# Routing four of five token tiles inside the last output product, with picks by counting, in a bidirectional RWKV-7 / GLA / expert trunk

## The reference, cut to what matters

```
x  = x + ga1 * (concat(y_rw, y_gla) @ w_out)
h2 = rmsnorm(x, norm2_g) * (1 + sc2) + sh2
g_logits = h2 @ moe_w_group + moe_b_group        # 4 groups
e_logits = h2 @ moe_w_expert + moe_b_expert      # 16 experts, 4 in a group
g_idx = argmax(g_logits); g_w = softmax(g_logits)[g_idx]
top_v, top_i = top_k(softmax(e_logits[group g_idx]), 2)
wts = g_w * top_v / sum(top_v)
x = x + ga2 * sum over the 2 picks of wts * (silu(h2 @ w3) * (h2 @ w1)) @ w2
```

## Time and profile before

| | us |
|---|---|
| median of 3 runs | 957.44 |
| lowest, highest of them | 954.83, 959.0 |
| span of the profiled execution | 963.3 |

### The profile page before, as it was taken

How to read it: one execution, slowest core, us unless ns; L and a number is a source line. 1 busy time by engine, 2 the same in 40 slices (tenths; PEclk the granted TensorE clock), 3 DMA queues, 4 the chain that set the end, 5 groups by cost and what they waited for, 6 DMA issues and landing times.

```text
span 963.3 us, 21505 instructions
## 1 busy us (share of the span) xinstructions
PE 868.1 (90%) x8900; PEld 533.8 (55%) x8900; DVE 562.5 (58%) x935; ACT 331.8 (34%) x583; POOL 151.6 (16%) x296
## 2 busy tenths in 40 slices
PE   2899999999999979888888988899976899999995
PEld 1455455666455436577777877545565444444442
DVE  3424046699986899365665656686244255444467
ACT  3231111142035664566666553122110122222223
POOL 7000111112000106122223420000001000000041
PEclk9999999999999989899999999999955899999998
DMA  9902222224253102112212121961019499999956
GB/s 331 378 23 95 94 88 99 89 88 154 75 188 109 67 1 42 26 21 53 39 37 34 32 38 47 314 254 44 22 54 361 133 328 373 367 371 368 327 126 226
DMA packets 120816, 142.46 MB, mean 148 GB/s; under 512 B 49996, under 2 KB 86280, under 8 KB 120328
## 3 DMA queue, kind: packets, MB, share of 16 engines
q1 hardware_dynamic: 111880, 116.55, 36.9%
q0 software_dynamic: 3744, 13.63, 4.5%
q10 hardware_dynamic: 5088, 10.82, 3.0%
HBM read 122.99 MB, written 18.00 MB: 146 GB/s over the span
## 4 chain that ended last, share of the span: by engine, by line
PE 79%; DVE 10%; DMA 5%; issue 3%; ACT 3%; SPq 0%; ACTq 0%; DVEq 0%; POOLq 0%
PE bank L1972 72%; PE bank L1976 7%; DMA region<-in_w_ada_dram 3%; DVE rk_r L1431 1%; ACT region L949 1%; DMA region<-in_w_in_dram 1%; DMA rk_r<-h_rows_dram,slot_tokens 1%; DVE region L1431 1%; DVE rk_r L1432 1%; DVE cl_b L1890 1%; DVE region L1961 1%; ACT w_sb L949 1%; ACT ada_row_buffers L949 0%; DVE region L1957 0%; DVE region L1943 0%
## 5 line engine op out<-in xcount | busy, mean ns | idle before, releaser
L1972 PE MATMUL bank<-region 64*64 64x64 f32 (+3 forms) x3900 | 402.6, 299 | 16.4 <-issue 6.5
L1972 PEld LDWEIGHTS bank<-region 64*64 64x64 f32 (+1 forms) x3900 | 233.3, 149 | 171.6 <-issue 160.1
L949 ACT ACTIVATE region<-bank 128x256 f32<-128x256 f32 (+3 forms) x216 | 97.8, 453 | 357.7 <-PE bank L1972 261.1
L1972 PE MATMUL bank<-region,rk_r 128*128 128x512 f32 x176 | 81.0, 615 | 0.8 <-issue 0.8
L1976 PE MATMUL bank<-ident,region 128*128 128x128 f32 (+2 forms) x403 | 63.6, 289 | 15.1 <-DMA region<-in_c_dram 11.1
L1976 PEld LDWEIGHTS bank<-ident,region 128*128 128x128 f32 (+2 forms) x403 | 46.0, 146 | 33.6 <-issue 24.0
L1942 DVE TENSOR_SCALAR region<-region 128x256 f32<-128x256 f32 x16 | 4.7, 295 | 101.3 <-ACT region L949 101.3
L1431 DVE SCALAR_TENSOR_TENSOR rk_r<-region,vec,rk_r 128x512 f32<-128x512 f32 x64 | 50.1, 783 | 11.1 <-ACT rk_r L949 9.0
L1972 PEld LDWEIGHTS bank<-region,rk_r 128*128 128x128 f32 x176 | 34.0, 198 | 40.2 <-issue 39.0
L924 POOL DMA_INDIRECT rk_r<-h_rows_dram,slot_tokens x16 | 15.2, 949 | 248.9 <-PE bank L1976 132.8
L1972 PE MATMUL bank<-scratch,region 64*64 64x64 f32 (+1 forms) x688 | 43.8, 232 | 6.3 <-issue 3.4
(11 more groups left out here) (279 smaller groups left out, 1149.0 us busy)
## 6 DMA issues: line engine op xcount, KB each, us to landing
region<-in_moe_w_dram SPq DMA_DIRECT2D x38, 1024.0 KB, 10.2
region<-in_w_ada_dram SPq DMA_DIRECT2D x12, 2048.0 KB, 9.0
region<-in_w_in_dram SPq DMA_DIRECT2D x6, 2048.0 KB, 9.1
cl_b<-in_moe_w_dram SPq DMA_DIRECT2D x10, 1024.0 KB, 12.6
expert_rows_dram<-yg_b ACTq DMA_DIRECT2D x14, 512.0 KB, 6.8
region<-late_condition_dram SPq DMA_DIRECT2D x3, 1024.0 KB, 9.4
a_rows_dram<-region SPq DMA_DIRECT2D x20, 128.0 KB, 2.7
region<-inverse_rows_dram SPq DMA_DIRECT2D x20, 128.0 KB, 3.1
```

The costliest lines, as they stand in the source:

```text
L949: return act.activation(out, in_, func, **kw)
L1972: return pe.matmul(out, lhsT, rhs, start=start, stop=stop)
```

## The change

1. **Tile order** is now [0, 3, 2, 1, 4].
2. **Shift's routing product.** POOL multiplies the routing weights by the columns of sh2 (`shift_w`, two operations), and PE multiplies them by a ones matrix: 8 products of 128x40, placed in the second tile's round (n = 1). VectorE reads bank `rc` there, and each tile's logits come out complete.
3. **Four tiles first.** In the last tile's round PE turns and routes the third and fourth tile between parts of `out` (4, 0); the four tiles' ranks are counted in the middle of `out` (4, 1), and most of their token products stand right behind it. x1, its transposes and h2 of the last tile come in two halves. Ranks, one-hot rows and ids of the last tile follow.
4. **Picks by counting** (`choose`). Each logit is compared with the others of its group (two comparisons, `beats`), masked so that ties go to the lower index, and summed. A logit beaten by none is first, one beaten by one is second.
5. **Weights of the picks** (`chosen_weights`, `pick_weights`, bank `sw`) come after the token numbers: VectorE works them out behind `slot_tokens`, PE forms `sw` within expert 0, after `turn_rows(1)`.
6. **Loads.** Weights of expert 1 start when `out` (4, 0) is done, those of expert 2 after the first three gathers have landed; w2 of expert 0 when the last mixer rows are turned. Buffers 2 and 3 are exchanged in w13 and in w2r. POOL's last gathers wait for `ug` 14, not 13.

The core of the diff:

```diff
@@ buffers
-        w13 = [ring[:, 1], ring[:, 0], cl_b[:, 0:SLAB].rearrange("p (k n) -> p k n", k=KT)]
+        w13 = [ring[:, 1], cl_b[:, 0:SLAB].rearrange("p (k n) -> p k n", k=KT), ring[:, 0]]
-              [region1[:, i * FT * D:(i + 1) * FT * D].rearrange("p (f n) -> p f n", f=FT) for i in range(2)]
+              [region1[:, i * FT * D:(i + 1) * FT * D].rearrange("p (f n) -> p f n", f=FT) for i in (1, 0)]
@@ sync
+            for n in range(NT - 2):
+                store_h2(n)
             wait_filled(sp, "yT", NT - 1, 1)
+            load_down(0)
             sp.dma_start(fg, final_g.partition_broadcast(P)).then_inc(s_fg, 16)
+            store_h2(NT - 2)
+            wait_filled(sp, "out", NT - 1, 0)
+            load_up(1)
+            load_down(1)
+            store_h2(NT - 1)
+            for j in range(3):
+                sp.wait_ge(s_xg[j], 16)
+            load_up(2)
+            wait_filled(sp, "router", NT - 1)
+            load_down(2)
@@ gpsimd
-                wait_filled(pool, "ug", LE - 1 if r == 0 else i)
+                wait_filled(pool, "ug", LE if r == 0 else i)
@@ vector
+            def choose(span):
+                own(TT(wins[:, :, :, 0], other, mine, ALU.is_ge))
+                own(TT(wins[:, :, :, 1], other, mine, ALU.is_gt))
+                own(TT(flat, flat, bc(before, 1, q), ALU.mult))
+                own(dve.tensor_reduce(out=R["beaten"]..., axis=AXX, op=ALU.add))
+                own(TS(R["hg"][:, a_:b_], R["beaten"][:, a_:b_, 0:NG], 0.0, None, ALU.is_equal))
+                tell(STT(per_group(picked_v[:, a_:b_]), experts, 2.0, group, ALU.is_lt, ALU.mult), s_pick)
+                own(STT(per_group(R["o1"][:, a_:b_]), experts, 0.0, group, ALU.is_equal, ALU.mult))
+                own(STT(per_group(R["o2"][:, a_:b_]), experts, 1.0, group, ALU.is_equal, ALU.mult))
...
+            router_logits(NT - 3)
             router_logits(NT - 2)
+            choose(FIRST)
+            residual(NT - 1, ((0,),))
+            scaled_rows(NT - 1, (0,))
+            ids_of(FIRST)
+            ranks(FIRST, ("rank", 0), False)
+            residual(NT - 1, ((1,),))
+            last_columns()
+            scaled_rows(NT - 1, (1,))
+            router_logits(NT - 1)
+            choose(LAST_T)
+            ids_of(LAST_T)
             h2_rows(NT - 1)
+            ranks(LAST_T, ("rank", 1), True)
@@ tensor
-                pe.wait_ge(s_wr, 64)
+                pe.wait_ge(s_shw, 1)
-                        ins = mm(b[:, c * NR:(c + 1) * NR], modv[:, 3 * KT + k, c:c + 1].broadcast_to([P, P]), wr[:, k, :], start=k == 0, stop=k == KT - 1)
+                    ins = mm(b[:, 0:2 * NR], ones, shift_w[:, k].rearrange("p c n -> p (c n)"), start=k == 0, stop=k == KT - 1)
...
+            out_half(n, 0, b0, range(0, 2))
+            turn_x1(n - 1)
+            router(n - 2)
+            out_half(n, 0, b0, range(2, 6))
+            router(n - 1)
+            finish(out_half(n, 0, b0, range(6, KT)))
+            out_half(n, 1, b1, range(0, 4))
             pe.wait_ge(s_pick, 1)
...
+            out_half(n, 1, b1, range(4, 6))
+            turn_x1(n, (0,))
+            finish(out_half(n, 1, b1, range(6, KT)))
```

More of the change, by code:

```diff
@@ new lines, in ids_of, with ranks @@
+            def ids_of(span):
+                a_, b_ = span
+                for o_, ids in (("o1", first_ids), ("o2", second_ids)):
+                    own(TT(ids[:, a_:b_], R[o_][:, a_:b_], bc(tokid[:, a_:b_], 2, NE), ALU.mult))
+            by_pick = lambda v: v.rearrange("p (j t) -> p j t", j=2)
+            def ranks(span, key, last_span):
+                a_, b_ = span
+                wait_filled(dve, *key)
+                rank = bank(key)[:, 0:(b_ - a_) * NE].rearrange("p (t n) -> p t n", n=NE)
+                for j, o_ in enumerate(("o1", "o2")):
+                    ins = TT(rtmp[:, a_:b_], rank, R[o_][:, a_:b_], ALU.mult)
+                    out_of(ins, *key) if j == 1 and not last_span else own(ins)
+                    own(dve.tensor_reduce(out=by_pick(R["rk"])[:, j, a_:b_], in_=rtmp[:, a_:b_], axis=AXX, op=ALU.add))
+                for j in range(2):
+                    ins = TT(onehot[:, j, a_:b_], bc(iota, 1, b_ - a_), bc(by_pick(R["rk"])[:, j, a_:b_], 2, P), ALU.is_equal)
+                    own(ins) if j == 0 else tell(ins, s_oh)
@@ L2600, in _ @@
-            for back in range(2, NT + 1):
-                ins = mm(b[:, back * NE:(NT + 1) * NE], ones, picked[:, 0:(NT + 1 - back) * NE], start=False, stop=back == NT)
-            finish(ins)
+            n = NT - 1
+            for j in range(2):
+                wait_result(pe, "yT", n, j)
+            b0 = open_early("out", n, 0)
+            out_half(n, 0, b0, range(0, 2))
[3 more added lines that the diff above has]
+            router(n - 1)
@@ new lines, in _ @@
+            open_bank("out", n, 0)
+            finish(out_half(n, 0, b0, range(6, KT)))
+            b1 = open_early("out", n, 1)
+            out_half(n, 1, b1, range(0, 4))
+            pe.wait_ge(s_pick, 1)
+            b = open_bank("rank", 0)
+            mm(b[:, 0:(NT - 1) * NE], upper, picked[:, 0:(NT - 1) * NE], start=True, stop=False)
+            for back in range(1, NT - 1):
+                ins = mm(b[:, back * NE:(NT - 1) * NE], ones, picked[:, 0:(NT - 1 - back) * NE], start=False, stop=back == NT - 2)
@@ new lines, in _, with token_ids @@
+            finish(ins)
+            br_ = open_early("rank", 1)
+            both = br_[:, 0:2 * NE].rearrange("p (s n) -> p s n", s=2)
+            for t in range(NT - 1):
+                mm(both, ones, bc(picked_v[:, t], 1, 2), start=t == 0, stop=False)
+            out_half(n, 1, b1, range(4, 6))
+            turn_x1(n, (0,))
+            open_bank("out", n, 1)
+            finish(out_half(n, 1, b1, range(6, KT)))
+            def token_ids(b, j, t):
+                return mm(b[:, 0:NE], onehot[:, j, t], (first_ids if j == 0 else second_ids)[:, t], start=(j, t) == (0, 0), stop=(j, t) == (1, NT - 1))
@@ new lines, in _ @@
+            pe.wait_ge(s_oh, 1)
+            bi = open_early("ids", 0)
+            for j in range(2):
+                for t in range(NT - 1):
+                    token_ids(bi, j, t)
+            turn_x1(n, (1,))
+            router(n)
+            pe.wait_ge(s_pick, 2)
+            open_bank("rank", 1)
+            mm(br_[:, 0:NE], upper, picked[:, (NT - 1) * NE:NT * NE], start=False, stop=False)
+            finish(mm(br_[:, NE:2 * NE], ones, picked[:, (NT - 1) * NE:NT * NE], start=False, stop=True))
```

282 lines of the change are left out of this document (144 added, 138 removed).

## The result

| | before | after |
|---|---|---|
| median | 957.08 (4 runs, 954.83 to 959.0) | 940.16 (4 runs, 937.97 to 942.05) |
| ratio, 95% interval | | 0.9827 (0.9802 to 0.9852) |
| span of the profiled execution | 963.3 | 937.0 |

16.9 us less; the forecast was 939.8. The two profiled spans lie 26.3 apart, though. The profiled run of before is itself a long one, 963.3 against a median of 957.08. 6.3 of the 26.3 stands ahead of the output stage: the load of x_prompt, which SP issues at the end of the scans, went out at 615.38 before and at 609.12 after. Zero is again the first instruction of the last tile's output product.

A forecast was written before the change was run, and what follows sets the result against it. PE's chain from the last output product to expert 0, mostly routing, was taken as the bound. Terms 1.9 + 20.9 + 14.0 + 4.3 + 2.8 = 43.9 against 61.5 gave -17.6, so 939.8 us from the median 957.44; range 935.5 to 946.0.

The forecast's parts named there:

- What bounds: PE's chain from the last output product to expert 0: 61.5 us, of which 47.7 is routing, nearly all at the lower clock.
- Shift's product, +1.9: Moved to the second tile's round, 16 narrow instructions at the full clock add 1.9 us ahead of zero; before, 6.99.
- Inside the last product, 20.9: Last tile's output product: 13.8 us of wide work plus 7.1 of inserted narrow work, ending 20.9 after zero.
- Slack: VectorE's lead inside the last product: the four tiles' picks ready 1.3 us before PE asks for them.
- the two ends for the four-dimensional operands: VectorE's picks of four tiles: 3.3 us at the lower end; large operations taking double add 2.6 at the upper.
- After it, 14.0: From the last product's end to the gather's issue, one line of ids, transposes, router, picks, ranks and ids: 14.0 us.
- Gather, 4.3: First gather, issue to landing, with the weight loads out of its way: 4.3 us, upper bound 8.1.
- `sw` at no cost: Slot weights' product within expert 0: 20 narrow instructions, about 2.3 us, fit PE's wait with 2.6 free.
- Second dip: Clock drop slowing expert 1's product to 8.58 us; its going would give 0 to -1.7, taken as 0.
- Clock inside the product (0.12): Rival: the clock falls inside the last output product, costing +9.2 at most; 944 to 949 us, chance 0.12.
- The forecast of -17.6: Stretch up to expert 0, shift's product included: 43.9 us where 61.5 was, so -17.6.

The follow-up runs named there:

- e1: Kernel before with only the shift's routing product changed: 16 instructions in the second tile's round instead of 32 behind the fourth router product; 952.01 us, ratio 0.9939.
- e5: Changed kernel with the last output product uninterrupted on PE, the four tiles' transposes, router products and ranks behind it; 952.47 us, ratio 0.9935.
- b0: Kernel before, unchanged, run once more for a second trace; 958.44 us.
- e10: Changed kernel, unchanged, run again for a second trace; 945.23 us, ratio 0.986 to the kernel before.
- e3: Changed kernel with picks found by maxima as before, instead of by counting; 943.71 us, ratio 0.9837.
- e2: Changed kernel with the weights of experts 1 and 2 issued just ahead of the gather, as before, behind the last h2 store; 944.95 us, ratio 0.9857.
- e4: Changed kernel with the product of the slot weights (`sw`) placed ahead of expert 0; 948.42 us, ratio 0.9886.
- e11: Changed kernel with `out` (4, 0) in one piece and the third and fourth tiles' transposes and router products piled up behind it; 943.94 us, ratio 0.9858.
- e7: Changed kernel with three useless wide products (128x512) on PE in the wait for the first gather; 940.36 us, ratio 0.9799.
- e9: Changed kernel with h2 of the last tile before its logits and nine useless wide products in PE's waits behind the last output product; 939.66 us, ratio 0.9795.

## Why the prediction was right

**What bounds.** Right. The line from the last product to expert 0 was the place: every part that an experiment took off or put on alone moved expert 0 in the trace, but only e1 and e5 moved the median beyond doubt. Nothing behind expert 2 changed (191.1 us from its start to the end before, 191.2 after).

**Shift's product, +1.9.** Right: +1.6, and +2.1 between b0 and e10. The gain behind zero was booked as 7.0; e1 shows about 1 more, since it also postponed the clock's fall for the transposes.

**Inside the last product, 20.9.** 20.5, with no wait and the clock at 1.00. Slack was to be 1.3 and is 1.5. Of the two ends for the four-dimensional operands the trace took the lower one exactly, and e3 says that it hardly mattered: even with picks by maxima the product ends within 0.1 of after's. That the overlap pays mostly by the clock (e5) the prediction did not say; it booked the narrow work at the full clock and asked only whether it would stay.

**After it, 14.0.** 13.3. Term by term, forecast and measured: ids 1.8, 1.7; transposes, wait and copy 1.75, 1.6; router product 2.3, 2.2 (clock falling inside it, as read; 1.93 to 2.95 in the other traces, so the place was partly luck); logits and picks 2.2, 1.9; order, h2, ranks, one-hot rows 3.7, 3.7; ids, cast, issue 2.25, 2.2.

**Gather, 4.3.** 4.4, and e2 gives 8.2 with the queue's order undone: cause shown. The Trainium skill (DMA: Bandwidth & Descriptors, Anatomy of one DMA) would have 3.2, as estimated ahead; no gather here took that. Even with the engines half idle (share 0.51) it was 4.4, and the shortest of all gathers in all traces was 4.2.

**`sw` at no cost.** Right: it fits into PE's wait, of which 0.61 is left. It saves nothing against before, where the gather hid it; e4 shows that ahead of expert 0 it would now cost 4.8.

**Second dip.** Taken as staying. It stayed away in after, but in b0 as well, so neither "it stays" nor "it may go, since PE idles less" describes it; it varies from run to run.

**Clock inside the product (0.12).** It did not come, and e11 shows that even 4.4 us of narrow work in one piece between wide products did not bring it.

**What the sum missed.** The forecast of -17.6 met the median's -16.9, but this is partly luck, since two errors cancel. By the traces from the load of x_prompt to the end the change takes 18.0 off between b0 and e10, neither of which has the dip, and 18.3 between before and after without the dip's 1.7. That is 0.4 to 0.7 more than forecast, mostly the stage itself (41.0 for 42.0). Against it stands the 1.1 outside the span that comes with the picks by counting (e3), a term that the sum does not have. Together they make the -16.9. On e10's chip the medians give only -13.5, 3.4 short of that; 3.0 of it is that e10's traced run, 942.24, lies so far below its median, that is, the kernel's own runs spread.

The time ahead of the load moves too, from 605.88 to 615.38 between traces (before 615.38, b0 610.14, e1 605.88; after 609.12, e10 610.98, e3 614.71). The clock there varies as well (380 to 400 us: 0.76 in e10, 0.79 in before, 0.91 in after and e5) but doesn't explain it, since e5 with 0.91 has 612.77 and e10 with 0.76 has 610.98. Corrected for how far each traced run lies from its median, it is 608.6 in the mean of the three traces with the old order of tiles and 611.7 in that of the eleven others. These were mostly taken on other chips, however; the two on the chip of b0 and e1 give 610.4. Whether the change does something there or the spread of a few runs makes that, no run here settles; e1, with the shift's two POOL operations, has the shortest, so these are not it.

**The parts don't add up.** e1 (7.6 to 8.1), e5 (10.9), e2 (4.1) and e3 (2.1) make some 25 us, against the 20.5 by which expert 0 moved. Each was measured alone, and the clock's fall stands in both e1 and e5; a split of the 20.5 into shares is not shown.

## What to carry to other kernels

Where PE stops being fed, lay the chain behind its last full stretch out as one line and ask of every step whether it needs the last tile; four fifths of this one did not, and leaving its work behind a product that PE does anyway, instead of inside it, cost 10.9 in the trace, more than half of that by the clock. Then look at what each queue holds when the one critical transfer is issued: with the weights of two experts issued just ahead of it the gather took 8.2, with one expert's sent early and the other's held back 4.4. Making VectorE's part cheaper paid (2.1) only for the tile whose picks nothing covers. And compare a run's time with its span in both kernels: 1.1 us of cost lay where no trace looks.

## What the runs showed of the hardware

**Narrow products alone didn't keep TensorE's clock here, and wide ones brought it back.** In before it fell to 0.50 while PE was busy without a gap; in e7 three wide products in a wait brought it back (0.66 over their four us, 1.00 behind them); in e9, with idle gaps of up to 1.3 us left but wide products in all waits, it stayed at 1.00 for 18 us. The Trainium skill (TensorE: Matmul & The Clock Gate, HAM oscillation) explains a fall by waits between bursts and advises to close them: e7 to e9 agree with the advice, before's busy row does not agree with waits as the only cause.

**Useless work can pay.** Three wide products in the wait for a gather brought expert 1 2.9 us forward in the trace (51.78 for 54.63). By medians e7 lies 0.3% below the change's first ratio, which its interval does not tell from it, and 0.6% below the second, which it does.

**One kernel, two ratios.** 0.9827 and 0.986 for the same code, with intervals that overlap. The stretch ahead of the change differs by 5.2 us between two traces of the kernel before and by up to 9.5 us over all traces, so two spans compared whole mislead, and the same event in both has to be the zero.
